# A hybrid attention and mixture-of-experts layer: a wait for constants moved, activation tables loaded ahead, and another order on VectorE at the shared expert's start

## What is computed

```python
x = layer_norm(DN_ALPHA * x + fox_mixer(x, ...), ln1_g, ln1_b)
scores = sigmoid(x @ w_router); sel = scores + router_bias
# best 4 of 8 groups by the sum of their two best, then the best 8 experts
grp_score = top_k(sel.reshape(T, 8, -1), 2)[0].sum(-1)
top_e = top_k(where(group_mask, sel, -inf), 8)[1]
w = scores[top_e] / sum(scores[top_e]) * 2.5
# every expert takes its tokens in blocks
y = scatter_add((silu(xb @ w_gate[e]) * (xb @ w_up[e])) @ w_down[e] * w)
shared = (silu(x @ ws_gate) * (x @ ws_up)) @ ws_down
x = layer_norm(DN_ALPHA * x + y + shared, ln2_g, ln2_b)
```

## Time and profile before

| what | us |
|---|---|
| median of three runs | 1742.29 (1742.08 to 1742.66) |
| the profiled execution's own time | 1759.47 |
| span in its trace | 1757.4 |
| TensorE busy (matmul) | 1592.9 (91%) |
| VectorE, ScalarE, Pool busy | 1186.9, 1025.6, 466.1 |
| attention ends, first norm begins | about 588 |
| residual of tile 7 | 713 |
| shared expert without a gap on TensorE from | 764 |
| TensorE's last matmul | about 1707 |

### The profile page before, as it was taken

One profiled execution on the slowest core, in us unless ns is written; L12 is line 12 of the kernel. 1 busy time (PEld: TensorE's weight loads), 2 busy tenths in 40 slices (PEclk: granted clock), 3 DMA queues, 4 the chain that ended last, 5 costly groups with the idle time before them and its releaser, 6 DMA issues.

```text
span 1757.4 us, 31696 instructions
## 1 busy us (share of the span) xinstructions
PE 1592.9 (91%) x8182; PEld 1304.8 (74%) x8183; DVE 1186.9 (68%) x2034; ACT 1025.6 (58%) x1692; POOL 466.1 (27%) x486
## 2 busy tenths in 40 slices
PE   6999999999998898799999999999999999999970
PEld 6897777777776777677777777777777777787750
DVE  3216677767777677737677787767777777778837
ACT  3215666566666544327566676666666667677733
POOL 0000000000000134432344344443454444444420
PEclk9999999999999998899999999999999999999985
DMA  7223222222224424558999999988998999999957
GB/s 229 89 83 85 60 67 48 60 54 60 66 48 133 161 87 146 182 202 290 283 275 291 296 361 342 296 244 265 321 300 247 290 330 292 364 335 343 363 130 286
DMA packets 161507, 369.24 MB, mean 210 GB/s; under 512 B 53040, under 2 KB 73520, under 8 KB 161456
## 3 DMA queue, kind: packets, MB, share of 16 engines
q1 hardware_dynamic: 136272, 284.21, 47.3%
q0 software_dynamic: 25184, 84.39, 19.2%
HBM read 294.39 MB, written 65.77 MB: 205 GB/s over the span
## 4 chain that ended last, share of the span: by engine, by line
PE 56%; issue 12%; DVE 11%; DMA 10%; ACT 7%; POOL 1%; DVEq 1%; another core or an unknown queue 0%; POOLq 0%; ACTq 0%; SPq 0%
PE bank L985 5%; PE bank L988 5%; PE bank L991 5%; DMA sums_scratch<-ys,sidx 4%; PE out_ps L1043 4%; PE out_ps L1044 3%; DMA x_rows<-rows_scratch,gidx 3%; PE out_ps L876 3%; PE q_ps L975 3%; PE k_ps L1020 3%; ACT probs L1216 3%; PE k_ps L1012 2%; PE k_ps L1013 2%; PE k_ps L855 2%; PE q_ps L85 2%
## 5 line engine op out<-in xcount | busy, mean ns | idle before, releaser
L1808 DVE TENSOR_TENSOR gu_lo<-raw_gu,gu_hi 128x1024 fp32r<-128x1024 f32 x260 | 306.7, 1221 | 20.0 <-ACT gu_hi L1324 18.2
L1324 ACT CAST gu_hi<-raw_gu 128x1024 fp32r<-128x1024 f32 x260 | 252.6, 1048 | 0.0
L985 PE MATMUL bank<-gu_hi,xb_hi 128*128 128x512 f32 x576 | 236.1, 410 | 2.5 <-ACT ex L1314 1.9
L988 PE MATMUL bank<-gu_lo,xb_hi 128*128 128x512 f32 x576 | 228.8, 397 | 0.0
L1227 ACT CAST pt_hi<-k_ps 128x512 fp32r<-128x512 f32 (+1 forms) x192 | 85.8, 482 | 123.1 <-PE k_ps L855 122.8
L1808 DVE TENSOR_TENSOR dn_lo<-raw_dn,dn_hi 128x1024 fp32r<-128x1024 f32 x130 | 154.5, 1209 | 0.5 <-ACT dn_hi L1324 0.5
L659 POOL DMA_INDIRECT sums_scratch<-ys,sidx x64 | 115.8, 1810 | 133.8 <-DMA sums_scratch<-ys,sidx 75.7
L991 PE MATMUL bank<-gu_hi,xb_lo 128*128 128x512 f32 x576 | 146.2, 395 | 0.0
L985 PEld LDWEIGHTS bank<-gu_hi,xb_hi 128*128 128x128 f32 x576 | 110.2, 191 | 27.1 <-issue 3.3
L1324 ACT CAST dn_hi<-raw_dn 128x1024 fp32r<-128x1024 f32 x130 | 129.6, 1047 | 0.0
L991 PEld LDWEIGHTS bank<-gu_hi,xb_lo 128*128 128x128 f32 x576 | 108.0, 187 | 26.4
(11 more groups left out here) (275 smaller groups left out, 3963.3 us busy)
## 6 DMA issues: line engine op xcount, KB each, us to landing
raw_gu<-in_moe_w_gate_dram SPq DMA_DIRECT2D x128, 512.0 KB
raw_gu<-in_moe_w_up_dram SPq DMA_DIRECT2D x128, 512.0 KB
raw_dn<-in_moe_w_down_dram SPq DMA_DIRECT2D x128, 512.0 KB
wqk<-in_fox_w_in_dram SPq DMA_DIRECT2D x66, 128.0 KB, 2.5
v_scratch<-v_out SPq DMA_DIRECT2D x32, 256.0 KB, 2.8
va<-v_scratch SPq DMA_DIRECT2D x16, 512.0 KB, 4.6
xs<-in_x_dram SPq DMA_DIRECT2D x8, 512.0 KB, 7.6
wv<-in_fox_w_in_dram SPq DMA_DIRECT2D x4, 1024.0 KB, 6.7
```

The lines of the kernel that those rows point to most:

```text
L985: i = pe.matmul(o3, xb_hi[s][:, c], g_hi[:, :, c], start=c == 0, stop=False, skip_group_check=True)
L988: pe.matmul(o3, xb_hi[s][:, c], g_lo[:, :, c], start=False, stop=False, skip_group_check=True)
L1324: a.copy(hi, raw).then_inc(S[done], 1)
L1808: dve.tensor_tensor(lo, raw, hi, ALU.subtract).then_inc(S[lo_ok], 1)
```

## The change

- `eps` is written without a wait; the wait for `c_const` now stands in tile 1, after its norm and ahead of `route(0)`.
- ScalarE gets a step `root_table`: a root of `eps` into a new column `eps_root` that nobody reads. It stands ahead of the first tile (behind `eps`), at the end of tiles 0 to 5, and once ahead of tile 7's norm. There `exp_of(6)` goes ahead of it and both ahead of the first block's `rows_hi`.
- On VectorE, `route(6)` moves from block 0 (ahead of `x1t_lo`, `dn_lo` and `ht_lo`) to block 1, ahead of that block's `hh`. `place(6)` and `place(7)` move from behind `rows_lo` to ahead of it, in blocks 1 and 2.

```diff
@@ scalar engine
+            def root_table():
+
+                a.activation(eps_root[:], eps[:], ACT.Sqrt)
+
+            act.wait_ge(S["var_ok"], 1)
+            root_table()
             for t in range(TT - 1):
                 std_of(t)
...
                 ax_of(t)
                 x1t_hi_of(t)
+                if t + 1 < TT - 1:
+                    root_table()
...
+            exp_of(TT - 2)
+            root_table()
             rows_hi(0, q_ps, "turned", 1, "rows_hi_ok")
-            exp_of(TT - 2)
             std_of(TT - 1)
@@ vector engine
-            dve.wait_ge(S["c_const"], 8)
             dve.memset(eps[:], LN_EPS / ALPHA ** 2).then_inc(S["var_ok"], 1)
             for t in range(TT - 1):
...
                 if t >= 2:
                     place(t - 2)
+                if t == 1:
+                    dve.wait_ge(S["c_const"], 8)
                 if t >= 1:
                     route(t - 1)
...
+                if b == 1:
+                    route(TT - 2)
                 h_of(b)
+                if b in (1, 2):
+                    place(TT - 3 + b)
                 rows_lo((b + 1) % 2, q_ps, "rows_hi_ok", b + 2, "rows_lo_ok")
 
                 if b == 0:
-                    route(TT - 2)
                     x1t_lo_of(TT - 1)
...
                 if b == 1:
-                    place(TT - 2)
                     route(TT - 1)
-                if b == 2:
-                    place(TT - 1)
```

More of the change, by code:

```diff
@@ L188, in build @@
                 eps = sb("eps", [P, 1], c=d)
+                eps_root = sb("eps_root", [P, 1], c=d)
                 ex = sb("ex", [P, 2, E], c=d)
```

## The result

The changed kernel takes 1736.2 us in median (1731.8 to 1745.1, 20 runs), the kernel before, run beside it, 1744.6 us (1742.1 to 1753.2, 20 runs). The ratio is 0.9949, with a 95% interval from 0.9937 to 0.9962: 8.9 us faster, or 0.5% (the medians are 8.4 us apart). All ratios leave out one run of before_third that took 1963.1 us at a granted clock of 0.745. The prediction said 1723.0 us and 1714 to 1733, so it was wrong: the direction was right, the size was less than half of the forecast. The measured median lies 3 us above the range, where the prediction had put rival C with a chance of 0.07.

A forecast was written before the change was run, and what follows sets the result against it. TensorE was taken as busy almost without a gap from 765 us on, so block 4's earlier start decides: 11.9 us up to tile 7's residual plus 7.5 us in the shared expert, 19.4 us off 1742.3, gives 1723 us, range 1714 to 1733.

The forecast's parts named there:

- rival C: Experts, near the limit of TensorE and DMA, give the earlier start back as waits for weights: 1735 to 1742 us; chance 0.07.
- Part 1: Tile 0: with the wait for Pool's constants moved, eps and the residual start 3.1 us earlier, at cost 0.
- Tiles 0 and 1: TensorE gains 3.90 us of idleness and 1.6 us of clock at tile 0, nothing more at tile 1: 5.5 us.
- Part 2: Norms: the root's table load, 1.28 us, leaves VectorE's path at tiles 0, 2 to 6 and 7; 5.1 us over tiles 2 to 5.
- Part 2 at tile 6: The root's 1.28 us passes through tile 6's routing weights and the rows' load to the residual of tile 7.
- Part 3: Shared expert's start: the new order on VectorE removes waits for dn_lo and tile 7's counts, 7.5 us net.
- tile 7's counts: Block 2: place right after hh lets the counts be read at once, 2.6 of 3.36 us, plus 1.6 us of clock.
- Price 0 to 3.2 us, plus the clock. I take 1.1: Block 3: cost of xb_lo standing behind place, whose last step waits for Pool's scatter to land; 1.1 us booked.
- I take no scale: The sum is taken unscaled off the 1742.3 us median, though the profiled execution was 17.2 us slower.
- A: New waits (slow landing at xb_lo) and lost clock in tiles 3 to 6 cost 4 to 9 us: 1727 to 1732 us; chance 0.24.
- B: More than the sum: tile 6's unexplained 5.00 us goes too, or the load costs more: 1714 to 1718 us; chance 0.15.
- D: Slower: row gathers meet weight loads worse; decides from 43 us of TensorE's waits for them, before 23.9; chance 0.03.

The follow-up runs named there:

- before_third: The kernel before, unchanged, run again for a third trace: 1743.9 us in median, ratio 0.9994.
- after_again: The changed kernel, unchanged, for a second trace on another chip: 1736.6 us in median, ratio 0.9952 against the kernel before.
- after: The changed kernel's first measurement and trace: 1736.2 us in median, ratio 0.9949 against the kernel before.
- after_third: The changed kernel, unchanged, for a third trace: 1735.1 us in median, ratio 0.9950 against the kernel before.
- after_fourth: The changed kernel, unchanged, for a fourth trace: 1741.7 us in median, ratio 0.9907 against the kernel before.
- split_place: Parts one and two with route(6) in block 1, and tile 7's place split, only its first two steps ahead of block 3's xb_lo: 0.9923 against the kernel before.
- f2_logits_hi_first: The changed kernel with the logits' eight x1t_hi matmuls ahead of the wait for x1t_lo: ratio 0.9954 against the kernel before.
- p2_table_ahead: The kernel before with the second part alone, the root's table loaded at each tile's end: ratio 0.9973.
- route_only_again: Second run of parts one and two with route(6) moved into block 1, places left behind rows_lo: ratio 0.9920 against the kernel before.
- p3_shared_order: The kernel before with the third part alone, the new order in the shared expert: ratio 0.9975.
- f1: The changed kernel with the last step of tile 7's place, which waits for the listing, behind block 3's xb_lo: 0.9932, then 0.9944, against the kernel before.
- before_again: The kernel before, unchanged, run again for a second trace: 1751.0 us in median, ratio 0.9992.

## Why the prediction was wrong, step by step

- **Part 1, 3.1 us: right at its place.** 3.90 to 0.72 us, 3.18 us, the same in all thirteen traces that have it. The factors were in time, and Pool's longest constant took 1.68 us beside VectorE's residual of 1.22 us, as long as alone (1.67 and 1.23); so "if the two exclude each other" fell, and on this the page "SBUF — State Buffer" of the Trainium skill (section "SBUF: two separate sides"), by which the residual goes free, agrees with the trace. By its runs this part alone gains nothing that shows (1.0005).
- **Tiles 0 and 1, 5.5 us with Part 1: right.** From tile 0's residual to tile 1's it took 14.12 us and takes 11.70: 2.4 us more than Part 1's 3.18, sum 5.6. The clock's 1.6 us in it were real: from the turning to the logits it takes 6.32 us in place of 7.87.
- **Part 2, 1.28 us a tile in tiles 2 to 5: right, as a floor.** In after_again the four take 15.10, 14.52, 14.53 and 14.51 us, in before_third 16.37, 15.78, 15.82 and 15.80: 5.1 us, the sum to the tenth. The price of the table, 1.28 us, stands. The Trainium skill, "ScalarE: Activation LUTs", section "What ACT_TABLE_LOAD costs", makes its 2.66 us of a load of about 1283 ns and a drain of about 1380 ns: every load in these traces shows the first, and the wait that went shows nothing of the second. With all parts the floor is not always reached: tile 3 takes 15.7 and 15.8 us in after and after_third, tile 5 takes 16.9 us in after_fourth.
- **Part 2 at tile 6, 1.28 us: wrong.** From its residual to tile 7's it took 23.1, 23.1 and 21.9 us and takes 23.0, 23.3, 22.0 and 23.4. In three of the four traces the gain of the root goes into a wait the prediction had not looked for: VectorE, now earlier, waits 1.60 us at `dest_i` of tile 4 for Pool's scatter (1.58 and 1.48 in after_again and after_third), ahead of the routing whose weights release the rows. These come 13.6 us after the tile's residual in after_again and 13.4 us in before_third. Pool's chain did not get faster. after_fourth has no such wait, and its weights come after 12.1 us; but the rows' load is issued 2.7 us after the weights' store, where it is 0.4 us in the other two, and why is open.
- **Part 3 and the shared expert's start, 7.5 us: wrong, and the term that missed by most.** S went from 54.1 to 57.5 us (three traces) to 51.9 to 53.1 (four): 3.3 us in the mean, 1.6 us against before_third. The wait for `dn_lo` (3.25 us) did go. Two items failed. The first is tile 7's counts, 2.6 us and 1.6 us of clock: the prediction took the 3.36 us for VectorE coming late, and gave them to the order. But VectorE's `xb_lo` made up only 1.42 us of them (749.93 to 751.35); for the next 1.41 us VectorE was itself idle, late behind the counts' record. With `place` ahead the wait is 0.57, 0.57, 0.57 and 2.10 us, in split_place 3.34; the old order has 0.57 us in before_third. The second is the new wait for `xb_lo`, "Price 0 to 3.2 us, plus the clock. I take 1.1": it came with 3.49, 1.91 and 3.60 us in three traces of the changed kernel (3.24 in f2_logits_hi_first), and only in the first did the eight matmuls behind it take 3.01 us (2.13 and 2.14 in the next two). The 1.1 us rested on a quicker landing; Pool saw the landing 5.06, 4.81 and 5.17 us after its last issue, as 5.19 before. In after_fourth TensorE stood for the counts instead.
- **"I take no scale": wrong as well.** The terms were read in one execution of 1759.5 us and taken off a median 17 us lower, without asking which of them a usual execution has. In S that is up to 3.4 us (57.5 against 54.1). In N it is not the sum that was too large: the late residuals that make 121.9 us out of 113.5 stand in no term. They are why the first pair of traces differs by 13.7 us in N, where the sum books 8.8 and before_third against after_again shows 6.2. The prediction noticed both the 17.2 us and the unexplained 5.00 us, but its reading that VectorE goes through tiles 2 to 6 without idle time held only for some of them: tile 4's residual had 2.14 us of it too. Where the kernel before has a median of 1758.3 us, the change brings it to 1741.7 us, near the forecast's own "1740.1 with the change". That is luck as far as is known: no trace of the kernel before was taken beside it, and the changed kernel's S there is 52.8 us, as in its other traces, so nothing points to Part 3's 7.5 us.
- **Rivals.** A (new waits) was right in its mechanism, 3.49 us at exactly its place, and wrong in its total, since it started from the same sum; its other half, lost clock in N, did not come in the changed kernel (0.96 to 0.97, where it was 0.91 to 0.95). Its rule that stops under 1 us were not followed by half clock fails in p2_table_ahead, where eight transposes took 1.97 us after a stop of 0.63 us. B fell for typical runs. C gave the right band by the wrong reason: E is 914.8 to 918.3 us in the changed kernel and 914.4 to 918.1 before, 916.0 in the mean of both, so nothing is given back that shows, and that all is passed on from block 4 was right in the mean (over all twenty traces E goes from 911.4 to 921.9 us). D has no trace: TensorE's waits for gathered rows are 25.9 us in place of 23.9, far from 43.

By stretches, in the mean of the traces: 3.2 us to tile 0, 117.6 to 108.3 in N, 55.8 to 52.5 in S, 15.8 us in all. The medians of the four comparisons give 8.4, 7.6, 10.8 and 16.6 us, 10.8 in the mean. The three traces of the kernel before all come from executions above their usual time or on a slow chip, so their mean is too high; with before_third alone the same sum gives 3.2 + 5.2 + 1.6 = 10.0 us, which agrees. Held against the forecast's 19.4 us, 3.5 of the missing 9.4 us lie ahead of tile 7's residual and 5.9 in Part 3.

What stays open: why VectorE goes on late behind TensorE's records. The granted clock explains only a part. In route_only_again the clock of N is 0.92, so 0.16 of its 115.9 us, 18.5 us, were at 1.2 GHz, and 9.3 us of matmuls were lost by it at most; N stands 8.8 us above 107.1, the lowest of any trace with parts one and two. p3_shared_order has nearly the same N and the same 0.92, so the same 9.3 us by this reckoning, and stands only 2.2 us above 113.5, the lowest of the old order. So how much of the slow time counts depends on where it falls, or on something else. No row names the releaser of the 5.00 us: in route_only_again the record of the last matmul into `q_ps` ends at 642.53 us, 3.9 us ahead of the residual that waits for it, as the counts' record does ahead of `pos`. Whether the result comes late or the record ends early, these traces don't tell. Whether f1 is faster than the changed kernel would take more runs.

## What to carry to other kernels

Before a sum is taken off a median, ask how the profiled execution stands to it. If it is slower by more than the gain that is sought, part of the waits in it belong to that execution: look which of the repeated stages (here eight tiles of the same work) take longer than the best of their kind, count the gain on the best one, and give the rest as the upper end of the range. Before a wait is booked to the order of the engine that ends it, look whether that engine was idle just then: if it was, another order frees nothing. A wait that comes from another engine's chain (a scatter and its landing) does not move when the engine in front of it becomes faster; price it at once for every place that arrives earlier, not only for the one that the diff moves. And a step that waits for a landing belongs behind, not ahead of, what TensorE needs next in the same queue.

## What was not expected of the hardware

- The same kernel's profiled executions reach block 4 at 759.9, 765.5 and 770.9 us with unchanged VectorE work. Time and granted clock of a run go together (correlation −0.71 to −0.94 over 6 to 35 runs of a kernel, −0.41 in one of six runs).
- The six comparisons here gave medians of 1744.2, 1744.6, 1745.9, 1752.0, 1753.7 and 1758.3 us for the kernel before. The gain was 0.5% in three of them and 0.9% in one.
- The turning of tile 0 took 1.97 us (1.2 GHz) after a stop of TensorE of 3.90 us, and 1.09 us (2.4 GHz) after one of 2.63 us. Elsewhere the same eight transposes took 1.97 us after 2.40 us (tile 6, kernel before) and after 0.63 us (block 0, p2_table_ahead), so the length of the stop ahead does not decide by itself.
- VectorE went on 0.04 us or 1.3 to 4.0 us after the end of the same record of TensorE's, in the same kernel in different executions (before_third and before_again).
- Useless matmuls went with a granted clock of 0.96 in a stage that had 0.91 to 0.95, and made nothing faster (0.9990, 0.9973 to 1.0008); VectorE's tiles there stayed 15.8 us apart.
